# Linear-attention items of a hybrid streaming encoder: silu, gates and rstd computed by other instructions and engines

## What is computed

```python
qa, ka, va, ga, qg, kg, vg, gg, lr = jnp.split(xn @ w_in, SPLITS, axis=-1)
log_a = jax.nn.log_sigmoid((lr @ w_gate_up + b_gate).astype(jnp.float32)) / GATE_TAU

def step(S, inp):                       # linear attention, block by block
    qc, kc, vc, ac = inp
    bcum = jnp.cumsum(ac, axis=1)
    diff = bcum[:, :, None] - bcum[:, None, :]
    decay = jnp.exp(jnp.where(causal[None, :, :, None, None], diff, -jnp.inf))
    att = jnp.einsum('bijhd,bjhd->bhij', qc[:, :, None] * decay, kc)
    o = (jnp.einsum('bhij,bjhe->bihe', att, vc)
         + jnp.einsum('bihd,bhde->bihe', qc * jnp.exp(bcum), S))
    ...

o_gla = rmsnorm(o_gla.astype(x.dtype), gla_norm_g).reshape(B, T, GLA_WIDTH)
mix = jnp.concatenate([o_attn * jax.nn.silu(ga), o_gla * jax.nn.silu(gg)], axis=-1)
return x + mix @ w_out
```

## Time and profile before

| what | us |
|---|---|
| median of 3 runs | 2008.53 (2007.07 to 2011.59) |
| the profiled execution | 2005.28 |
| its span, first to last instruction | 2003.5 |
| PE busy in it | 1909.5 (95%) |
| DVE busy | 946.7 (47%) |
| ACT busy | 566.5 (28%) |
| POOL busy | 499.4 (25%) |

### The profile page before, as it was taken

How to read it: one execution, slowest core, us unless ns; L and a number is a source line. 1 busy time by engine, 2 the same in 40 slices (tenths; PEclk the granted TensorE clock), 3 DMA queues, 4 the chain that set the end, 5 groups by cost and what they waited for, 6 DMA issues and landing times.

```text
span 2003.5 us, 29742 instructions
## 1 busy us (share of the span) xinstructions
PE 1909.5 (95%) x10432; PEld 1713.8 (86%) x10432; DVE 946.7 (47%) x1709; ACT 566.5 (28%) x1256; POOL 499.4 (25%) x445
## 2 busy tenths in 40 slices
PE   5999999989999999999999999999999999999999
PEld 4899999867777779999988888888999888888887
DVE  6445553133334431111277777776556554454433
ACT  6211111033333331000144443343001133343332
POOL 1433333211111222332344344333233100000000
PEclk8999999999999999999999999999999999999999
DMA  6322222322222223212323222224352465565454
GB/s 217 130 66 65 65 62 75 84 70 76 70 72 70 76 72 107 72 52 69 99 70 90 76 84 76 80 80 135 104 152 91 150 220 188 192 220 191 164 189 132
DMA packets 238059, 218.10 MB, mean 109 GB/s; under 512 B 16753, under 2 KB 202609, under 8 KB 236562
## 3 DMA queue, kind: packets, MB, share of 16 engines
q1 hardware_dynamic: 170370, 174.99, 27.8%
q10 hardware_dynamic: 67632, 42.36, 7.8%
HBM read 166.82 MB, written 52.31 MB: 109 GB/s over the span
## 4 chain that ended last, share of the span: by engine, by line
PE 76%; DVE 13%; issue 4%; ACT 3%; DMA 2%; ACTq 1%; DVEq 0%; POOL 0%; SPq 0%; POOLq 0%
PE p L1569 14%; PE p L1571 14%; PE p L1570 14%; PE p L1640 6%; PE p L1642 6%; PE p L1644 6%; DVE xn L1738 4%; PE p L521 2%; PE p L504 2%; ACT work L568 2%; PE p L730 2%; PE p L514 2%; DVE work L644 1%; DMA work<-h_t 1%; DVE work L630 1%
## 5 line engine op out<-in xcount | busy, mean ns | idle before, releaser
L1569 PE MATMUL p<-x_hi,w_lo 128*128 128x384 f32 x2112 | 731.7, 346 | 0.0
L1571 PE MATMUL p<-x_hi,w_hi 128*128 128x384 f32 x2112 | 709.3, 336 | 0.0
L1570 PE MATMUL p<-x_lo,w_hi 128*128 128x384 f32 x2112 | 708.8, 336 | 0.0
L1569 PEld LDWEIGHTS p<-x_hi,w_lo 128*128 128x128 f32 x2112 | 398.2, 189 | 41.2 <-issue 38.8
L467 POOL TENSOR_TENSOR w_hi<-raw,small 128x512 fp32r<-128x512 f32 x176 | 186.4, 1059 | 867.3 <-PE p L1571 856.0
L1570 PEld LDWEIGHTS p<-x_lo,w_hi 128*128 128x128 f32 x2112 | 398.6, 189 | 0.4
L1571 PEld LDWEIGHTS p<-x_hi,w_hi 128*128 128x128 f32 x2112 | 397.8, 188 | 0.0
L472 POOL TENSOR_TENSOR w_lo<-raw,w_hi 128x512 fp32r<-128x512 f32 x176 | 228.6, 1299 | 13.8
L1818 DVE TENSOR_TENSOR w_lo<-raw,w_hi 128x512 fp32r<-128x512 f32 x192 | 131.9, 691 | 202.7 <-ACT w_hi L1520 202.5
L1520 ACT ACTIVATE w_hi<-raw 128x512 fp32r<-128x512 f32 x192 | 120.6, 631 | 241.0 <-PE p L1644 212.9
L1640 PE MATMUL p<-w_hi,x_lo 128*128 128x512 f32 x576 | 162.9, 391 | 7.0 <-DVE w_lo L1818 7.0
(11 more groups left out here) (181 smaller groups left out, 1823.7 us busy)
## 6 DMA issues: line engine op xcount, KB each, us to landing
raw<-in_w_out SPq DMA_DIRECT2D x192, 256.0 KB, 3.0
raw<-in_w_in SPq DMA_DIRECT2D x176, 256.0 KB, 3.7
h_t<-xn SPq DMA_DIRECT2D x132, 192.0 KB, 1.9
work<-h_t ACTq DMA_DIRECT2D x42, 256.0 KB, 5.1
work<-h_t SPq DMA_DIRECT2D x24, 384.0 KB, 5.1
out<-work SPq DMA_DIRECT2D x36, 256.0 KB, 4.9
work<-h_t ACTq DMA_DIRECT2D x17, 512.0 KB, 5.6
work<-in_x_prompt SPq DMA_DIRECT2D x32, 256.0 KB, 5.1
```

Source lines behind the costliest of these rows:

```text
L1569: pe.matmul(out, w_lo[:, k, :], x_hi[:, k, tok], start=(k == 0), stop=False)
L1570: pe.matmul(out, w_hi[:, k, :], x_lo[:, k, tok], start=False, stop=False)
L1571: mm = pe.matmul(out, w_hi[:, k, :], x_hi[:, k, tok], start=False, stop=(k == KT - 1))
```

## The change

Six edits, all in items 29 to 44.

1. **Silu as one function.** ACT applies `Silu` to `acc[n]`, into `tmp_a` for groups 0 and 2 and `tmp_b` for group 1; DVE does the one product with the loaded output.
2. **Silu behind the level work.** A second order `item_late`, for items 29 to 37 on ACT and DVE, runs both units first and then the silus of groups 0 and 1, ahead of `unit[2]`.
3. **One table set for exp and ln**, asked for at the head of the gates.
4. **The inverse root on POOL** as a power of -0.5 (`linear_rstd`), behind the split of the next item's weights; the Newton step goes.
5. **The load of `lr`** for the next tile stands right behind the gates of this one.
6. **The loads of q and k** for the next tile stand ahead of the squares, behind a wait for the last level's products.

```diff
-                act.dma_start(lr[0:LRR, :], h_t[LR0:LR0 + LRR, cols]).then_inc(sl_lr, 16)
...
             def gates(self, t):
                 act = self.act
+                act.preload_act_table_set("natural_log_exp_and_others")
                 act.wait_ge(sl_log, t + 1)
...
-            def rstd(self, t):
-                act = self.act
-                act.wait_ge(sl_var, t + 1)
-                act.activation(l_rstd, l_var, ACT.Ln).then_inc(sl_lnv, 1)
-                act.wait_ge(sl_lnv, t + 1)
-                act.activation(l_rstd, l_rstd, ACT.Exp, scale=-0.5).then_inc(sl_rs, 1)
...
                 def part_0():
                     self.gates(t)
+                    self.load_lr(t + 1)
...
                 def part_2():
+                    self.act.wait_ge(sl_zz, NZ * t + NZ)
+                    self.load(t + 1)
                     self.squares(t)
-                    self.rstd(t)
-                    self.load(t + 1)
...
                 dve.wait_ge(sl_rs, t + 1)
-                dve.tensor_tensor(l_var, l_var, l_rstd, ALU.mult).then_inc(sl_nt, 1)
...
-                dve.tensor_tensor(l_rstd, l_rstd, l_var, ALU.mult).then_inc(sl_nt, 1)
-                dve.wait_ge(sl_nt, 4 * t + 4)
...
+        def linear_rstd(pool, t):
+            pool.wait_ge(sl_var, t + 1)
+            pool.tensor_tensor(l_rstd, l_var, mhalf[:, 0:1].to_broadcast([P, N_GLA]), ALU.pow).then_inc(sl_rs, 1)
...
                 linear_pool(pool, j - J_GLA, LEVELS, P)
                 split(pool, j + 1)
+                linear_rstd(pool, j - J_GLA)
...
             def item_silu(j, n):
                 wait_acc(act, j, n)
-                act.wait_ge(s_staged, j * NG + (n + 3))
-                act.activation(tmp_a, acc[n][:, 0:TN], ACT.Exp, scale=-1.0).then_inc(s_sig, 1)
+                act.wait_ge(s_staged, j * NG + (3, 2, 4)[n])
+                act.activation(tmp_silu[n], acc[n][:, 0:TN], ACT.Silu).then_inc(s_sig, 1)
...
+            def item_late(j, before, now, unit):
+                before(j - 1, 2)
+                unit[0]()
+                unit[1]()
+                now(j, 0)
+                now(j, 1)
+                unit[2]()
...
                     dve.wait_ge(s_sig, (j - J_GLA) * NG + (n + 1))
-                    dve.tensor_scalar(tmp_a, tmp_a, 1.0, None, ALU.add).then_inc(s_schain, 1)
-                    dve.wait_ge(s_schain, base + 1)
-                    dve.reciprocal(tmp_a, tmp_a).then_inc(s_schain, 1)
...
-                    dve.tensor_tensor(tmp_a[:, 0:m], acc[n][:, 0:m], tmp_a[:, 0:m], ALU.mult).then_inc(s_schain, 1)
-                    dve.wait_ge(s_schain, base + 3)
                     dve.wait_ge(s_gate[n], (j - J_GLA) * 16 + 16)
-                    done(dve.tensor_tensor(stage[n][:, 0:m], stage[n][:, 0:m], tmp_a[:, 0:m], ALU.mult))
+                    done(dve.tensor_tensor(stage[n][:, 0:m], stage[n][:, 0:m], tmp_silu[n][:, 0:m], ALU.mult))
...
-                item(j, silu, silu, linear.tile(j - J_GLA))
+                item_late(j, silu, silu, linear.tile(j - J_GLA))
```

More of the change, by code:

```diff
@@ L118, in project @@
         tmp_b = xn[:, 4 * TN:5 * TN]
+        tmp_silu = [tmp_a, tmp_b, tmp_a]
         banks = [ctx.enter_context(nc.psum_tensor(f"p1_{i}", [P, 512], F32)) for i in range(8)]
@@ L776, in __init__, with load_lr @@
                 self.act = act
+            def load_lr(self, t):
+                self.act.dma_start(lr[0:LRR, :], h_t[LR0:LR0 + LRR, ds(t * P + PAD, P)]).then_inc(sl_lr, 16)
             def load(self, t):
@@ L799, in first @@
                 act.dma_start(l_og[:, 0:2], consts[:, 0:2]).then_inc(sl_st, 16)
+                self.load_lr(0)
                 self.load(0)
@@ L1139, in part_0 @@
                                        ACT.Square, accum_out=l_ss[:, h:h + 1]).then_inc(sl_sq, 1)
-                    self.lin.rstd(T)
                 return part_0, lambda: self.lin.leave(T), lambda: None
@@ L1408, in _ @@
                 split(pool, j + 1)
+                linear_rstd(pool, j - J_GLA)
             linear_pool(pool, T, DEC_LEVELS, DEC_SEQ)
-            with pool.Fori(J_LEV + 1, 1 + N_ITEMS) as j:
+            with pool.Fori(J_LEV + 1, J_LEV + 2 + N_GLA) as j:
+                split(pool, j)
+            linear_rstd(pool, T)
+            with pool.Fori(J_LEV + 2 + N_GLA, 1 + N_ITEMS) as j:
                 split(pool, j)
@@ L1489, in _ @@
             linear.first()
-            item(J_GLA, nothing, item_silu, linear.tile(0))
+            item_late(J_GLA, nothing, item_silu, linear.tile(0))
             with act.Fori(J_GLA + 1, J_GLA + NTP) as j:
-                item(j, item_silu, item_silu, linear.tile(j - J_GLA))
+                item_late(j, item_silu, item_silu, linear.tile(j - J_GLA))
             decode = decode_act(act, linear)
-            item(J_LEV, item_silu, item_silu, decode.levels())
+            item_late(J_LEV, item_silu, item_silu, decode.levels())
             for h in range(N_GLA):
@@ L1732, in run @@
                 def run(j, n):
[L1733 removed]
                     m = min(TN, SEQ - n * TN) if prompt_only else TN
                     dve.wait_ge(s_sig, (j - J_GLA) * NG + (n + 1))
[L1736 to L1739 removed]
                     if m < TN:
                         staging_free(j, n)
[L1742 to L1744 removed]
+                        dve.tensor_copy(stage[n][:, m:TN], tmp_silu[n][:, m:TN])
                     dve.wait_ge(s_gate[n], (j - J_GLA) * 16 + 16)
[L1746 removed]
+                    done(dve.tensor_tensor(stage[n][:, 0:m], stage[n][:, 0:m], tmp_silu[n][:, 0:m], ALU.mult))
                 return run
@@ L1787, in _ @@
             linear.first()
-            item(J_GLA, plain, silu, linear.tile(0))
+            item_late(J_GLA, plain, silu, linear.tile(0))
             with dve.Fori(J_GLA + 1, J_GLA + NTP) as j:
-                item(j, silu, silu, linear.tile(j - J_GLA))
+                item_late(j, silu, silu, linear.tile(j - J_GLA))
             decode = decode_dve(dve, linear)
-            item(J_LEV, silu, silu_g, decode.levels())
+            item_late(J_LEV, silu, silu_g, decode.levels())
             for h in range(N_GLA):
```

6 lines of the change are left out of this document (removed).

## The result

The changed kernel takes 1960.56 us (median of 4 runs, 1959.03 to 1962.87), the kernel before 2008.19 us (4 runs, 2007.07 to 2011.59). The ratio is 0.9761, with a 95% interval from 0.9744 to 0.9778: 47.6 us less. The sign was right, and so were the waits that it said would go; the size was not. The profiled execution of the changed kernel took 1961.11 us, its span is 1959.3 us. Against the profiled execution of before (2005.28) that is 44.2 us.

A forecast was written before the change was run, and what follows sets the result against it. The prediction took TensorE (PE), busy 1909.5 of 2003.5 us, as the bound and counted only its waits: 16.6 + 5.1 + 3.1 + 3.8 + 2.2 - 0.2 + 3.1 + 3.3 = 37.0 us off 2008.53 gives 1971.5 us, range 1964 to 1982.

The forecast's parts named there:

- The outputs (L741): Output matmuls of the linear items: with the silu chain gone the merge ends before PE comes; 16.6 us go.
- The price of a stop: All through the sum: only PE's listed waits count, so each stop is priced at its listed idle time.
- an item some 3 us shorter: Check on the linear items: 2.08 + 0.24 + 0.5 us and a little, 1.7 more where the clock fell.
- The clock: Three falls to half clock behind waits ahead of L741 in the linear items go: 5.1 us, bounds 0 and 5.1.
- The load of `lr`: Logits wait (L693): load issued some 40 us ahead; 3.1 of 5.5 us go, the first item's 2.4 stay.
- The diagonal and the levels (L711, L730): PE's waits there go as Ln, the minimum and the level chain come sooner: 3.8 and 2.2 us.
- POOL's power: Inverse root on 128x4 takes 0.8 us; free in prompt items, 0.2 us of new wait in the decode's level item.
- Heads: First matmul of the decode heads: four waits behind the silu chain go, 3.1 us together.
- The projection: Start of the output projection: DVE's first low half starts sooner; 3.3 of PE's 6.17 us wait go.
- The wait at L741 didn't stay: Rival at the output matmuls: merge of level 6 as late as before, 16.6 + 5.1 us stay, 1993.2 us; chance 0.10.
- the clock didn't: Rival: the clock falls all the same because short idle spots remain; 5.1 us stay, 1976.6 us; chance 0.07.
- POOL didn't become the bound: Rival: POOL's power beyond 2.8 us is paid in nine items; at 8 us it gives 2018 us; chance 0.02.

The follow-up runs named there:

- the runs with 4, 5 and 7 reciprocals: Changed kernel with 4, 5 or 7 chained 128x128 reciprocals on DVE ahead of the last merge: 1967.09, 1983.76 and 2014.47 us.
- the early order: Changed kernel with the silu of group 0 back between the two units on ACT and DVE: 1962.53 us, ratio 0.9773.
- the later `lr` load: Changed kernel with the `lr` load of the next tile behind the squares again, as in the kernel before: 1958.33 us, ratio 0.9751.
- The run with that one line: Kernel before with silu as one function, the late order and the exp and ln set loaded ahead of the logits wait: 1966.93 us, ratio 0.9812.
- the run with the set and the old silu: Changed kernel with the old silu chain (exp on ACT, four DVE steps) in the early order, all else as changed: 2001.52 us, ratio 0.9969.

## Why the prediction fell short

By its own steps.

- **The outputs (L741).** Mechanism and margin right: the merge is done 1.6 us ahead of PE (1.0 to 2.0 said), the silus by 1102.4, the products 1.06 us together. The term was too small: 8 stops of some 2.08 us cost 2.34 each, 18.7 us, not 16.6.
- **The price of a stop is the step that failed.** "So I count only what PE waits for" was taken from the idle time in the list of waits, which leaves out 0.25 to 0.28 us at most of the stops (the table above, and the heads below). Items 30 to 36 together are 32.1 us shorter; their idle time was 20.4 and their two falls of the clock 3.4, so 8.3 us were left out there, and another 1.0 at the heads. At level 0 this was nearly all of the cost: 0.02 of idle time, 0.28 paid. Against it stand item 29, 2.5 us shorter where some 3.9 were booked (the next point), and the 1.25 us of the attention items. The forecast's own check, "an item some 3 us shorter", shows it at once: 4.09.
- **The clock.** All three falls that stood behind L741 went, and none came in their place: 1.71 us an item (46.60 less 44.89) in items 31 and 34, as booked. The third was in item 29, where it can't be told from the rest. What the sum missed has the other sign: in the first linear item the half clock lasts 6.83 us in the changed kernel (the row above), where it lasted 3.41 before, from 992.98, behind a wait of 2.78 instead of 2.39: some 2 us given back. It lasted 3.41 us there in the runs with 4, 5 and 7 reciprocals, with the early order and with the later `lr` load too, so it varies from execution to execution.
- **The load of `lr`.** The stops went, but the move that they were booked to was one of two reasons, each enough by itself. And 1.69 of the 3.1 us was one stop, that of item 37.
- **The diagonal and the levels (L711, L730)** went by the table set, but only beside the new silu. The run with that one line leaves no entry for the diagonal and 1.2 us of the levels'; the run with the set and the old silu keeps 5.1 us at the diagonal. The prediction had both reasons at the diagonal, and its sum needs both.
- **POOL's power** takes 1.02 us on 128x4, 0.8 said, between the bounds 0.55 and 2.2. With 0.55 for one column this makes some 0.16 us a column (an estimate from two shapes), so less of it is start than was booked. The view of its line (count, ns min/median/max), and one item on POOL, DVE and PE:

```profile
L1012 POOL TENSOR_TENSOR small<-small x9: 1014/1018/1029, 1035.2 to 1484.7; 128x4 f32<-128x4 f32 x9
```

```profile
1074.77 1.29 POOL L470 TENSOR_TENSOR w_lo<-raw,w_hi 128x512 fp32r<-128x512 f32 x1
1076.01 1.03 POOL L1012 TENSOR_TENSOR small<-small 128x4 f32<-128x4 f32 x1
```

```profile
1077.08 1.66 DVE L961 TENSOR_SCALAR work<-p,small 128x256 f32<-128x256 f32 x4 [2.36 <-POOL small L1012]
```

```profile
1079.38 0.82 PE L757 MATMUL p<-consts_sb,work 128*128 128x128 f32 x6
```

  DVE now waits 2.36 us for POOL, and in an item of the prompt nobody waits for DVE: its first piece is there by 1077.5, PE comes at 1079.38. In the decode's level item, where 0.2 us of new wait were booked, PE's transposes meet DVE's pieces (four in 1.66 us from 1321.84) and take 1.38 us, 1.03 before: 0.35 us.

```profile
1322.62 1.38 PE L757 MATMUL p<-consts_sb,work 128*128 128x128 f32 x8
```

- **Heads.** 3.1 said, 4.14 measured: four stops of 0.69 to 0.82 listed, 0.94 to 1.07 paid. The same step.
- **The projection.** 3.3 said, 3.14 measured, and the wait of 2.9 us that was named for it is 3.03:

```profile
1550.01 3.56 DVE L1817 TENSOR_TENSOR x_lo<-work,x_hi 128x768 fp32r<-128x768 f32 x4 [0.17 <-ACT x_hi L1513]
```

```profile
1559.99 1.22 PE L1644 MATMUL p<-w_hi,x_lo 128*128 128x512 f32 x2 [3.03 <-DVE w_lo L1824]
```

  DVE's first low half follows ACT's first high half (1549.14 there) after 0.87 us, as it would without the chain.
- **The rivals.** The wait at L741 didn't stay, the clock didn't, POOL didn't become the bound. The low end of the range lay too high for another reason: upward the range took in errors of whole terms, downward only the draw of the median and two small bounds. A common error of all the stops was in none of the rivals.

## What to carry to other kernels

On an engine that is busy nearly all the time, price a stop by start-to-start intervals of the instructions around it (against a place without a stop), not by the idle time that a wait list gives; with many short stops the difference was more than a quarter of the gain here (1.13 of the 4.05 us of item 33). Waits that stand in a row on one path are covered by one another: silu alone brought 18 us, the rest without it and without the late order 6, the whole 48, so a part that measures as worthless by itself may be the larger half of a change. Before a table of functions is replaced by another, count the loads that each engine order will need and put the one that remains where the engine waits anyway.

## What was not expected of the hardware

- A stop of PE at the outputs costs 0.29 us beyond its listed idle time of 0.94 us, 0.27 beyond 1.93 and some 0.22 beyond 3.84. At the logits of item 33 it was 0.07, so the extra isn't the same at every place.
- One stop an item lowered the granted clock in none of eight items at 0.94 us, in five at 1.92, and in all eight at 3.84, there for 6.83 us; in the kernel before, with its shorter stops beside, in three of eight at 2.0 to 2.1. So the price of a stop of about 2 us varies by 1.7 us from item to item.
- The silu product and POOL's split hold each other up in both directions. In items 38 to 44 of the changed kernel the product of group 2, on 128x256 there, began 0.04 us behind a POOL step of 1.04 us and took 1.28 us; the last one, at 1563.33 with POOL idle, took 0.42. In the item shown above it was POOL's step beginning at 1104.21, behind a product, that took 1.43 us instead of 1.04. "SBUF — State Buffer" of the Trainium skill, section "SBUF: two separate sides", has DVE with two SBUF inputs and GpSimd lock each other out for a whole instruction. The trace agrees that each is held up by the other; what each loses here, 0.86 and 0.39 us, is somewhat less than the other's whole time (1.04 and 0.55). POOL and DVE in item 38, then POOL in item 31:

```profile
1353.44 1.04 POOL L465 TENSOR_TENSOR w_hi<-raw,small 128x512 fp32r<-128x512 f32 x1
1353.49 1.28 DVE L1743 TENSOR_TENSOR xn<-xn 128x256 f32<-128x256 f32 x1
```

```profile
1104.21 1.43 POOL L465 TENSOR_TENSOR w_hi<-raw,small 128x512 fp32r<-128x512 f32 x1 [0.44 <-PE p L1575]
```
